# Decoder trunk on one core: the attention weights of three head pairs turned by VectorE in 32x32 blocks instead of by TensorE

## The reference

```python
def block(args):
    qa, qb, i = args
    s1 = einsum('bqhd,bkhd->bhqk', qa, k1) * scale
    s2 = einsum('bqhd,bkhd->bhqk', qb, k2) * scale
    a = causal_softmax(s1, i, S) - lam * causal_softmax(s2, i, S)
    return einsum('bhqk,bkhe->bqhe', a, v)
```

## Time and profile before

| | us |
|---|---|
| median of 3 runs | 2020.8 (2020.62 to 2021.06) |
| profiled execution | 2021.03 |
| its span | 2019.2 |
| around the span | 1.83 |
| TensorE busy | 2010.2 |
| VectorE busy | 1503.3 |
| ScalarE busy | 978.8 |
| median from issue to landing of a 1 MB load of QKV weights | 5.2 |

### The profile page before, as it was taken

One profiled execution on the slowest core, in us unless ns is written; L12 is line 12 of the kernel. 1 busy time (PEld: TensorE's weight loads), 2 busy tenths in 40 slices (PEclk: granted clock), 3 DMA queues, 4 the chain that ended last, 5 costly groups with the idle time before them and its releaser, 6 DMA issues.

```text
span 2019.2 us, 26207 instructions
## 1 busy us (share of the span) xinstructions
PE 2010.2 (100%) x9302; PEld 1681.7 (83%) x9302; DVE 1503.3 (74%) x2169; ACT 978.8 (48%) x1263; POOL 10.5 (1%) x21
## 2 busy tenths in 40 slices
PE   9999999999999999999999999999999999999998
PEld 8888888888888888888888998888888888888887
DVE  7687798887468558757888787988558757855875
ACT  7555555544344444434446665554444434433443
POOL 0000000000000000000000000000000000000000
PEclk9999999999999999999999999999999999999999
DMA  8645554656555655655565544565655555565563
GB/s 308 222 152 181 187 167 167 207 191 206 187 189 186 208 187 187 207 187 187 182 214 169 142 149 146 193 224 188 208 188 187 202 193 187 174 218 189 168 218 115
DMA packets 218034, 381.98 MB, mean 189 GB/s; under 512 B 15600, under 2 KB 40560, under 8 KB 217968
## 3 DMA queue, kind: packets, MB, share of 16 engines
q1 hardware_dynamic: 217104, 379.03, 56.7%
q10 hardware_dynamic: 864, 2.10, 0.3%
HBM read 379.00 MB, written 2.10 MB: 189 GB/s over the span
## 4 chain that ended last, share of the span: by engine, by line
PE 84%; issue 15%; POOL 0%; DVE 0%; POOLq 0%; DVEq 0%; ACT 0%
PE acc L472 27%; PE acc L474 27%; PE acc L473 27%; PE acc L747 1%; PE acc L748 1%; PE acc L749 1%; PE side L800 0%; PE side L790 0%; PE side L773 0%; PE side L802 0%; PE side L779 0%; PE side L781 0%; PE side L782 0%; PE side L780 0%; PE side L783 0%
## 5 line engine op out<-in xcount | busy, mean ns | idle before, releaser
L1358 DVE TENSOR_TENSOR wlo<-raw,whi 128x1024 fp32r<-128x1024 f32 (+2 forms) x700 | 836.3, 1212 | 372.7 <-ACT whi L894 369.4
L894 ACT ACTIVATE whi<-raw 128x1024 fp32r<-128x1024 f32 (+2 forms) x700 | 725.6, 1048 | 706.0 <-PE acc L474 676.0
L472 PE MATMUL acc<-whi,opB 128*128 128x512 f32 x1296 | 505.5, 390 | 0.0
L474 PE MATMUL acc<-whi,opB 128*128 128x512 f32 x1296 | 504.4, 389 | 0.0
L473 PE MATMUL acc<-wlo,opB 128*128 128x512 f32 x1296 | 504.2, 389 | 0.0
L472 PE MATMUL acc<-whi,opA 128*128 128x512 f32 (+2 forms) x1296 | 502.4, 388 | 0.0
L474 PE MATMUL acc<-whi,opA 128*128 128x512 f32 (+2 forms) x1296 | 501.1, 387 | 0.0
L473 PE MATMUL acc<-wlo,opA 128*128 128x512 f32 (+2 forms) x1296 | 500.9, 387 | 0.0
L474 PEld LDWEIGHTS acc<-whi,opB 128*128 128x128 f32 x1296 | 243.3, 188 | 50.5
L472 PEld LDWEIGHTS acc<-whi,opB 128*128 128x128 f32 x1296 | 243.3, 188 | 50.4 <-DVE wlo L1358 0.3
L473 PEld LDWEIGHTS acc<-wlo,opB 128*128 128x128 f32 x1296 | 243.4, 188 | 50.1
(11 more groups left out here) (254 smaller groups left out, 1112.3 us busy)
## 6 DMA issues: line engine op xcount, KB each, us to landing
raw<-in_w_up SPq DMA_DIRECT2D x128, 1024.0 KB, 5.4
raw<-in_w_down SPq DMA_DIRECT2D x128, 1024.0 KB, 5.1
raw<-in_a_w_qkv SPq DMA_DIRECT2D x44, 1024.0 KB, 5.2
raw<-in_a_w_o SPq DMA_DIRECT2D x16, 1024.0 KB, 5.1
raw<-in_b_w_o SPq DMA_DIRECT2D x16, 1024.0 KB, 5.2
raw<-in_w_ukv SPq DMA_DIRECT2D x32, 256.0 KB, 4.4
raw<-in_w_dkv SPq DMA_DIRECT2D x4, 1024.0 KB, 5.3
raw<-in_b_w_dq SPq DMA_DIRECT2D x4, 768.0 KB, 5.0
```

Source lines behind the costliest of these rows:

```text
L472: mm(o, a_hi, w_hi, start=first and c == 0, stop=False)
L474: done = mm(o, a_lo, w_hi, start=False, stop=last and c == chunks - 1)
L894: done = fn(whi[:, place:place + ch, 0:n], raw[:, r, c0:c0 + ch, 0:n], ACT.Copy)
L1358: done = tt_(wlo[:, place:place + ch, 0:n], raw[:, r, c0:c0 + ch, 0:n], whi[:, place:place + ch, 0:n].bitcast(F32), ALU.subtract)
```

## The change

For the weights of the first three pairs, TensorE's transposes are left out. VectorE turns them, in 32x32 blocks, from `attn` to the SBUF tile `attnT`, which existed already and was used in the second layer alone. One instruction takes 32 query rows and 32 of every 128 keys of both heads, which is 6 blocks or 32 partitions x 192 elements; there are 16 for a pair. They stand in VectorE's Q block in four groups of four: behind the splits of halves 6 and 7, and of halves 0 and 1 of the K block. ScalarE's high part and VectorE's low part then read `attnT` in SBUF instead of the PSUM banks. The fourth pair stays as it was.

```diff
@@ TensorE, qkv
                 block_tok(b + 1, 1, p, opA, urgent=True, aside={2: x_sum_squares} if first else {
-                    1: lambda: transpose_attn(2 * prev, 2, 4 * prev + 4),
                     4: lambda: da_values(prev, 4 * prev + 4)})
@@ ScalarE
-            def copy_attnT(heads_before, b0, dst):
+            def copy_attnT(p, turned):
                 for h in range(2):
-                    act.wait_ge(attnT_done, heads_before + h + 1)
-                    fn(dst[:, h, :], side[b0 + h][:, 0:KEYS], ACT.Copy).then_inc(attnT_ready, 1)
+                    act.wait_ge(attnT_done, 2 * p + h + 1)
+                    fn(attnT_hl[:, 0, h, :], turned[h][:, 0:KEYS], ACT.Copy).then_inc(attnT_ready, 1)
...
-                    4: lambda: copy_attnT(2 * pv, 2, attnT_hl[:, 0]),
+                    4: lambda: copy_attnT(pv, [attnT[:, h, :] for h in range(2)]),
@@ VectorE
+            def attn_turn(p, tokens):
+
+                dve.wait_ge(attn_ready, 4 * p + 4)
+                for a in tokens:
+                    for c in range(4):
+                        rows, cols = (slice(32 * k, 32 * k + 32) for k in (a, c))
+                        done = nc.vector.transpose(
+                            attnT[cols].rearrange("p h (k n) -> p (h k) n", k=3)[:, :, rows],
+                            attn[rows].rearrange("p h (k n) -> p (h k) n", k=3)[:, :, cols])
+                if 3 in tokens:
+                    done.then_inc(attnT_done, 2)
+
+            def da_attnT_lo(p, turned):
...
-                    tt_(attnT_hl[:, 1, h, :], side[2 + h][:, 0:KEYS], attnT_hl[:, 0, h, :].bitcast(F32),
+                    tt_(attnT_hl[:, 1, h, :], turned[h][:, 0:KEYS], attnT_hl[:, 0, h, :].bitcast(F32),
                         ALU.subtract).then_inc(attnT_lo, 1)
...
-                    body(b, {4: lambda: da_weights(pv)}, end=10)
+                    body(b, {4: lambda: da_weights(pv), 6: lambda: attn_turn(pv, (0,)), 7: lambda: attn_turn(pv, (1,)),
+                             8: lambda: attn_turn(pv, (2,)), 9: lambda: attn_turn(pv, (3,))}, end=10)
                     rope_qk(p, 0)
```

More of the change, by code:

```diff
@@ L1125, in squares_and_scale @@
                 o_scale(last)
-            body(B_WO, {4: lambda: copy_attnT(2 * last, 2, attnT_hl[:, 0]), 6: squares_and_scale, 7: lambda: o_hi(last, both(0))})
+            body(B_WO, {4: lambda: copy_attnT(last, side[2:4]), 6: squares_and_scale, 7: lambda: o_hi(last, both(0))})
             def out_proj(b0, uses, v0, gain):
@@ L1587, in k_low @@
                 tt_(k_lo, both(2), k_hi.bitcast(F32), ALU.subtract).then_inc(qkT_lo, 1)
-            def da_attnT_lo(p):
+            def attn_turn(p, tokens):
[9 more added lines that the diff above has]
+            def da_attnT_lo(p, turned):
                 for h in range(2):
                     dve.wait_ge(attnT_ready, 2 * p + h + 1)
-                    tt_(attnT_hl[:, 1, h, :], side[2 + h][:, 0:KEYS], attnT_hl[:, 0, h, :].bitcast(F32),
+                    tt_(attnT_hl[:, 1, h, :], turned[h][:, 0:KEYS], attnT_hl[:, 0, h, :].bitcast(F32),
                         ALU.subtract).then_inc(attnT_lo, 1)
@@ L1674, in weights_lo_and_turn @@
                 def weights_lo_and_turn():
-                    da_attnT_lo(pv)
+                    da_attnT_lo(pv, [attnT[:, h, :] for h in range(2)])
                     q_turn(p, (1,))
@@ L1726, in mean_and_scale @@
                 o_scale(last)
-            body(B_WO, {3: lambda: da_weights(last), 4: lambda: da_attnT_lo(last), 6: mean_and_scale,
+            body(B_WO, {3: lambda: da_weights(last), 4: lambda: da_attnT_lo(last, side[2:4]), 6: mean_and_scale,
                         7: lambda: o_lo(last, both(0))})
```

## The result

| | before | changed |
|---|---|---|
| median of 22 runs each, us | 2021.01 | 2023.84 |
| lowest and highest | 2020.37, 2021.85 | 2023.39, 2026.12 |
| span of the profiled execution, us | 2019.2 | 2021.6 |

The ratio is 1.0014, with a 95% interval from 1.0008 to 1.002. The changed kernel is 2.8 us slower. That is above the 2022.9 at which my range ended.

A forecast was written before the change was run, and what follows sets the result against it. A chain over VectorE, GpSimd and ScalarE was taken to decide when TensorE proceeds. 2021.03 - 0 + 0.06 = 2021.1 us, less 0.23 for the runs' median, gave 2020.8; range 2018.8 to 2022.9.

The forecast's parts named there:

- The chain to half 2 of the V block: VectorE, GpSimd and ScalarE, 175.5 to 200.1 us: as long as TensorE's own way, not entered by its transposes.
- the idle time before the rope: VectorE's idleness, 3.94 us in pair 2 and 3.79 in pair 3, as cover for its transposes; cost 0.
- the wait at half 4: VectorE's wait for ScalarE, 0.46 us in pairs 1 and 2, 0.62 in pair 3; takes up 0.19 us lateness.
- rival B: Low parts in the chain take 482 ns from SBUF, not 547; three pairs give 0.4 us: 2020.4; chance 0.05.
- Gain by this step: 0: TensorE comes to half 2 of the V block 0.66 us sooner and waits 0.66 longer; bounds 0 to 1.98 us.
- C: VectorE's transposes, 0.448 us each, overrun their cover, losing 2.1 us: 2022.9; chance 0.12, beyond 4.04 us 0.03.

The follow-up runs named there:

- the third experiment: Changed kernel with VectorE's `o_scale` moved ahead of the split of half 0 of the V block, right behind `o_means`; 2021.38 us, ratio 0.9999.
- Turned twice: Changed kernel with TensorE's six transposes put back in pairs 1 to 3, output unused, beside VectorE's; 2021.55 us, ratio 1.0.

## Why the prediction was wrong

**Right.** Six transposes cost TensorE 0.66 us a pair, and they're spared. The chain to half 2 of the V block binds, so none of it reaches the end: the third experiment, which only takes the collision away, lands at 0.9999. VectorE's transposes take 370 ns where I worked out 369 and lie under the idle time before the rope. I had VectorE 0.19 us late there in pairs 2 and 3; it is 0.04, and the wait at half 4 takes it up. Turned twice shows them free. Low parts out of SBUF take about as long as out of PSUM: two in 1.02 us, after 1.01, and not 0.13 less, so rival B falls. With it falls, for this instruction, the difference between PSUM and SBUF that the Trainium skill gives in "VectorE: DVE Perf Modes", in its section on the TRN2 errata; the instruction's other input, the high part, was in SBUF both times.

**Wrong.** The step that failed is "Gain by this step: 0", by its reason: "The pieces in between (values, squares of the output) come 0.66 us sooner, but VectorE's order behind half 4 doesn't wait for them: `oms` is bound by the split ahead of it." It holds for `oms`, and I didn't follow the order one row on. The split behind `oms` did wait for ScalarE, 0.32 us, behind those same squares. When the wait went, its place in time against GpSimd's `ors` was reversed, and `ors` grew from 1.01 to 1.91 us: 0.9 us a pair in a link that I had counted as fixed. That is 2.7 us; the medians are 2.8 apart. I asked only what coming sooner could gain, and not what it would start earlier.

The price of such a collision stood in the trace of the kernel before. GpSimd's `rs` of 128x2 numbers, the same operation as `ors`, begins there 0.16 us behind a VectorE split and takes 1.62 us; `lrs`, of 128x2 numbers too, takes 0.69 with nothing of VectorE beside it:

```profile
38.09 1.22 DVE L1358 TENSOR_TENSOR wlo<-raw,whi 128x1024 fp32r<-128x1024 f32 x1
38.25 1.62 POOL L431 TENSOR_TENSOR rs<-xms,neg_half 128x2 f32<-128x2 f32 x1 [35.85 <-DVE xms L1508]
...
1104.26 0.69 POOL L443 TENSOR_TENSOR lrs<-lms,neg_half 128x2 f32<-128x2 f32 x1 [6.59 <-DVE lms L1834]
```

That is 0.93 us more behind a split, about what `ors` loses.

None of the rivals had this. C came nearest with its 2022.9, and by another cause: VectorE overrunning its cover, which these runs exclude. Had the range reached the 2023.84 by its bound, that would have been luck.

## What to carry to other kernels

Where an engine is made earlier, list every instruction that thereby starts earlier, not only those that end the chain. A short wait in another engine's order (here 0.32 us) may be the gap in which a third engine's small, critical instruction runs. And time taken off the busiest engine comes through only when the next link gives way too: here the same change was worth +2.8 us alone, and -2.6 to -2.8 us with one or two pieces of the programs in another order.

## What the runs showed of the hardware

GpSimd's power of 128x4 numbers takes 1.01 us when it starts 0.25 us before a VectorE subtraction of two SBUF tiles, and 1.91 us when it starts 0.17 us behind one of 1.22 us; it then ends 0.86 us after the subtraction does. In the first case the subtraction isn't longer (1.23 us). VectorE's transposes of SBUF tiles, 0.44 us each, the first of which began 0.05 us before it, don't lengthen it at all (1.01 us).

A collision isn't always dear. In the trace of the kernel before, a power of 128x2 numbers that starts 0.17 us behind a VectorE instruction of only 0.28 us, which reads two SBUF tiles as well, takes 0.70 us, as long as one alone (0.69). That fits a loss that depends on how much of VectorE's instruction is left, but no run varied it:

```profile
1096.81 0.28 DVE L1352 SCALAR_TENSOR_TENSOR wlo<-raw,gains_x,whi 128x64 fp32r<-128x64 f32 x1
...
1096.98 0.70 POOL L431 TENSOR_TENSOR rs<-xms,neg_half 128x2 f32<-128x2 f32 x1 [789.26 <-DVE xms L1415]
```

The Trainium skill has this in "SBUF — State Buffer", under "Who interferes with whom": a VectorE instruction with two SBUF inputs contends with a GpSimd instruction that reads SBUF, one with at most one SBUF input, outside the modes that use both ports, does not, and the order of issue decides who is blocked. The trace agrees in the first two points, and in the third where VectorE was first. Where GpSimd was first, by 0.25 us, the trace shows neither of them blocked: 1.01 us and 1.23 us. Whether it is the second input or the kind of instruction that matters, these runs don't tell apart; a subtraction with one input in PSUM beside `ors` wasn't tried.
